# Input products of the state-space branch in single-pass form, from operands split into two parts and stacked to 128 rows through memory

## The chip, the cores and the metric

The kernel runs on one core of a Trainium2 chip. Its engines run in parallel, each in its own program order, and wait for one another on semaphores: TensorE (PE in the profile; its weight loads are PEld), VectorE (DVE), ScalarE (ACT), GpSimd (POOL), and SyncE (SP), which here only issues DMAs. The metric is the device time of one execution in microseconds, lower is better; all times below are in us where nothing else is said.

## The reference

Two transformer-like blocks in float32 run one after the other over 256 tokens with a model width of 2048. The second has three branches: a gated mixer, a state-space branch ("s5") and an attention in stick-breaking form. Their gated sum goes through an output projection, and an MLP of width 8192 follows. The change is in the s5 branch only. It has 64 groups of 16 input channels, each driving 64 complex states:

```python
def s5_mixer(xin, ...):
    u = xin.reshape(bsz, seq, 64, 16)
    ...                                   # a = exp(lam * dt), discretised factors k
    bb_re = k_re[..., None] * b_re - k_im[..., None] * b_im
    bb_im = k_re[..., None] * b_im + k_im[..., None] * b_re
    bu_re = jnp.einsum('blgh,gph->blgp', u, bb_re)
    bu_im = jnp.einsum('blgh,gph->blgp', u, bb_im)
    ...                                   # s[t] = a * s[t-1] + bu[t], complex
    y = (jnp.einsum('blgp,ghp->blgh', s_re, c_re) - jnp.einsum('blgp,ghp->blgh', s_im, c_im))
    y = y.reshape(bsz, seq, 1024) + d * xin
    g = jax.nn.gelu(y)
    return g * jax.nn.sigmoid(g @ w_glu + b_glu)
```

## The kernel before

**Units.** All weight matrices stream through in units: `plan` lists chunks of 512 columns, a chunk has 2 to 8 units, and a unit is 256 rows of weights (512 KB) times 256 tokens. The kernel has 1048 units. For each, SP loads it into `raw` (L377), ScalarE copies it rounded into `whi` (`hi`, L616), VectorE subtracts to get the rest, `wlo` (`lo`, L1121), and TensorE runs 12 matmuls of 128x512 (`unit`, L1735): high by high, high by low and low by high parts, each in a single-pass type (fp32r). All three buffers are rings of four units. SP's load of a unit waits until the split of the unit four before is done, ScalarE's copy waits until TensorE has used the unit four before, and TensorE waits for the split. So the copies and splits run at most four units ahead of TensorE, and the loads four further.

**The order around them.** Everything else is written as generators (`Steps`) that yield a position. On each engine the branch work of position p runs right behind that engine's part of unit p (counted from the first unit of the block's phase), in the order of the list of generators. A position is a place in each engine's program, no time: one engine reaches it earlier than another. In block 2, positions 0 to 95 are the input projections, and the s5 input is ready in two halves: stages are moved by ScalarE (`stage_moves2`, from position 12 and 20 on) and turned by VectorE (`stage_turn2`, positions 20 and 28).

**The s5 branch.** The 32 tiles of 128 states (two groups each) run in 16 pairs m, every `S5D` = 5 positions from `S5Q` = 26. On TensorE `s5_in` (L1878) multiplies at position 26 + 5m: for both parts r (real, imaginary) and both tiles e of the pair, 32 rows of B by 32 rows of the turned input, 256 tokens, in full float32 (which the trace shows as two records a matmul), at the row tile where the operands lie:

```python
ins = mm(PU[e][:, T * r:T * r + T], BT[r][c:c + 32, i, :], XI[c:c + 32, i, :],
         tile_position=(c, 0))
```

VectorE then rotates and scans tile j (`s5`, L1524 to L1532) at `s5_place(j)`: 29 + 5m for the first of a pair and 30 + 5m for the second, behind its split of that unit. It waits for `bu_mm`, which `s5_in` raises. GpSimd rotates back (`block2`, L522 to L525). `s5_out` (L1896) multiplies four tiles of states by C at positions 41 + 10i, so right behind `s5_in` of m = 3, 5 and so on to 15, and once more at 111. SP loads a rotation table for each tile at positions 25 and 30 + 5k (`tables`, L388). From position 72 to 110 the stick-breaking attention runs in the same stage (`attn2`): a head takes 5 positions and goes back and forth between TensorE, ScalarE and VectorE. B is read from memory by GpSimd's queue at the end of block 1, into `BT`. C is scaled by GpSimd (L507 to L512).

Of the kernel before, what the change touches and what calls it, by code (L numbers as in the profile page):

```python
# [21 lines left out]
P = 128  # L22
T = 256
# [26 lines left out]
def build(nc, A, out):  # L50
    with ExitStack() as ctx:
# [197 lines left out]
        BT = [slot(Z, 2 + r).rearrange("p (i c) -> p i c", i=8) for r in range(2)]  # L249
# [21 lines left out]
        GLUQ = [8, 9, 11, 12]  # L271

# [100 lines left out]
        def _(sp_):  # L373
# [6 lines left out]
            def tables():  # L380

                for j in range(S5_TILES):
                    yield S5Q + S5D * (j // 2) + (4 if j % 2 else -1) if j >= NTAB else 6 + j
                    if j == 0:
                        sp_.wait_ge(S("tables_saved"), 32 * S5_TILES // TG)
# [15 lines left out]
            for b in blocks:  # L401
                branch = Steps(tables() if b == 2 else iter(()))
                for ph in "ab":
                    for ch in plan[b, ph]:
                        for i in range(ch.nu):
                            if ch.u0 + i == 0:
                                load_first(ch)
                            else:
                                load(0, ch.u0 + i, ch.w[:, UK * i:UK * i + UK, ch.col:ch.col + CH])
                            if ch.n == 0 and i < 7:  # L410
                                load_pair(i + 1)
                            if 6 <= ch.u0 + i < 6 + NCH:
                                load_x(ch.u0 + i - 6)
                            branch.upto(ch.u0 + i - u0[b, "a"])
                up = rows("w_mlp_up" if b == 1 else "w_mlp_in_2")
# [21 lines left out]
        def _(pool):  # L437
# [46 lines left out]
            def block2():  # L484

                pool.wait_ge(used, mlp_base(1, NF - 1))
                for r in range(2):
                    pool.dma_start(BT[r], A["b_t"][r]).then_inc(S("s5_b_in"), 16)
                for r in range(2):
                    pool.dma_start(CT[r], A["c_t"][r]).then_inc(S("s5_c_in"), 16)  # L490
                pool.dma_start(GW, A["gm_w_t"]).then_inc(S("gm_w_in"), 16)
                pool.wait_ge(evict["dve"], down0[1] + NF * NCH)
                pool.dma_start(A["x1"].rearrange("(t p) n -> p t n", p=P), X).then_inc(S("x_saved"), 16)
                pool.wait_ge(S("gm_w_in"), 16)
# [9 lines left out]
                pool.wait_ge(S("s5_c_in"), 32)  # L504
# [8 lines left out]
                for j in range(S5_TILES):  # L513
# [13 lines left out]
                    if j in (24, 25, 26):  # L527
                        pool.wait_ge(S("z_mm"), 4)
                        if j == 24:
                            pool.dma_start(GMG, A["gm_norm_g_2"][0].partition_broadcast(P)).then_inc(S("gm_gain_in"), 16)  # L530
                        else:
                            load_bias(0, j - 25)
# [4 lines left out]
            def make_tables():  # L537
# [3 lines left out]
                for g in range(S5_TILES // TG):  # L541
                    c, s = TNEW
                    if g:
                        pool.wait_ge(S("tables_saved"), 32 * g)
# [16 lines left out]
                    for i, m in enumerate(TNEW):  # L561
                        pool.dma_start(A["tables"][TG * g:TG * g + TG, :, i, :].rearrange("j p t -> p j t"), m)\
                            .then_inc(S("tables_saved"), 16)
                pool.wait_ge(S("tables_saved"), 32 * S5_TILES // TG)
# [13 lines left out]
            for bi_, b in enumerate(blocks):  # L578
# [4 lines left out]
                if b == 2:  # L583
                    load_biases(3, 5)
                    pool.wait_ge(S("x_saved"), 16)
# [21 lines left out]
        def _(act):  # L607
# [122 lines left out]
            def evictions(b):  # L730
# [4 lines left out]
                for ch in plan[b, "a"] + plan[b, "b"]:  # L735
# [31 lines left out]
                    elif tag == "glu":  # L767
                        act.wait_ge(S("gm_T"), 4)
                        staged(ch, ST[h])
                    else:  # L770
                        if b != blocks[0] and stages == 0:
                            act.wait_ge(S("x_saved"), 16)
# [145 lines left out]
            def s5a():  # L918

                yield S5Q + 88  # L920
                act.wait_ge(S("s5_y"), 8)
                a(GS, GS, ACT.Gelu_apprx_tanh).then_inc(S("s5_g"), 1)
                for h in range(2):
                    yield S5Q + 89 + h
                    act.wait_ge(S("s5_g"), 1)
                    a(YH[:, 8 + 4 * h:12 + 4 * h, :], GS[:, 4 * h:4 * h + 4, :]).then_inc(S("s5_g_hi"), 1)
# [182 lines left out]
        def _(dve):  # L1109
# [446 lines left out]
            def gmlp():  # L1556
# [6 lines left out]
                dve.wait_ge(S("gm_gain_in"), 16)  # L1563
# [17 lines left out]
            def s5_g_lo():  # L1581
                for h in range(2):
                    yield S5Q + 90 + h
                    dve.wait_ge(S("s5_g_hi"), h + 1)
                    tt(YL[:, 8 + 4 * h:12 + 4 * h, :], GS[:, 4 * h:4 * h + 4, :],
                       YH[:, 8 + 4 * h:12 + 4 * h, :].bitcast(F32), ALU.subtract).then_inc(S("s5_g_split"), 1)
# [10 lines left out]
            def mlp(b):  # L1597
# [57 lines left out]
                if b != blocks[-1]:  # L1655
                    dve.wait_ge(S("tables_saved"), 32 * S5_TILES // TG)
# [22 lines left out]
            def gained():  # L1679
                for n in range(2):  # L1680
                    yield (-3, 0)[n]
                    if n == 0:
                        dve.wait_ge(S("gain_in"), 16)
# [6 lines left out]
            for b in blocks:  # L1690
                gens = [Steps(g) for g in (([down_adds(b - 1)] if b != blocks[0] else []) + [x_lo(b, "a"), norm(b, "a"), evictions(b)] + (
                    [stage_turn(), attn1(), attn1_y(), lru(), pool(), sconv(), s5_params()] if b == 1 else [stage_turn2(), s5(), attn2(), s5_g_lo(), gmlp(), glu_out()]) + [merge_turn(b), merge_lo(b)])]
# [38 lines left out]
        def _(pe):  # L1731
# [336 lines left out]
            for b in blocks:  # L2068
# [5 lines left out]
                for ch in plan[b, "a"] + plan[b, "b"]:  # L2074
# [6 lines left out]
                    if ch.tag[0] == "glu":  # L2081
                        pe.wait_ge(S("s5_g_split"), 2)
# [21 lines left out]
def laid_out(v, np):  # L2104
# [18 lines left out]
    m["b_t"], m["c_t"] = bt.reshape(2, P, 8, P), ct.reshape(2, P, 8, P)  # L2123
# [23 lines left out]
```

## Time and profile before

| | us |
|---|---|
| median of 3 runs | 2961.64 |
| lowest and highest | 2961.48 and 3687.77 |
| the profiled execution | 2961.87 |
| its span, from first to last instruction | 2960.1 |
| granted TensorE clock, mean | 1.000 |

The profile is one execution. A row of its timeline has the start, the duration, the engine, the source line, the operation, the names of the written and read tiles, the shape and how many in a row were merged; in brackets stands for how long the engine had been idle and what ended it. Matmuls are pipelined, so the distance of two starts, not the duration, is what one costs. Position p of block 2 is unit p in what follows; its start is the first of its 12 matmuls.

### The profile page before, as it was taken

The numbers are of one execution on the slowest core, as the hardware profiler recorded it, in microseconds if no ns is written. First come the engines' busy times: TensorE is split into PE (matmuls) and PEld (weight loads), VectorE is DVE, ScalarE is ACT, GpSimd is POOL, SyncE is SP. The second block draws the span as 40 slices with busy tenths as digits, with TensorE's granted clock in tenths as the row PEclk, the third lists the DMA queues.
The fourth block names the chain that finished last, engine by engine and source line by source line (L and its number), as shares of the span: only waits on it lengthen the run. The fifth ranks groups of instructions, "written<-read, shape, count | busy, mean of one in ns | idle before, by whom it ended". The sixth has DMA issues, their size and how long they took to land.

```text
span 2960.1 us, 37410 instructions
## 1 busy us (share of the span) xinstructions
PE 2947.3 (100%) x13302; PEld 2429.1 (82%) x13302; DVE 1978.9 (67%) x2104; ACT 1732.3 (59%) x2455; POOL 440.4 (15%) x422
## 2 busy tenths in 40 slices
PE   9999999999999999999999999999999999999998
PEld 7888888888888888888887788888888888888887
DVE  6767654566667777676778886555556666666666
ACT  6776644547655555555675576554557554555555
POOL 1000110110035243320235450110000000000000
PEclk9999999999999999999999999999999999999999
DMA  8656666756666676666765555766665666666664
GB/s 257 182 162 194 198 203 195 199 179 205 191 192 221 191 223 198 217 220 191 261 192 198 194 187 163 217 209 210 203 205 185 200 192 193 193 194 192 192 192 162
DMA packets 298845, 588.43 MB, mean 199 GB/s; under 512 B 18465, under 2 KB 18481, under 8 KB 298353
## 3 DMA queue, kind: packets, MB, share of 16 engines
q1 hardware_dynamic: 292352, 563.61, 61.6%
q0 software_dynamic: 5952, 22.77, 2.4%
q8 instruction: 66, 1.08, 0.1%
q10 hardware_dynamic: 432, 0.62, 0.1%
q14 instruction: 43, 0.34, 0.0%
HBM read 574.35 MB, written 12.58 MB: 198 GB/s over the span
## 4 chain that ended last, share of the span: by engine, by line
PE 95%; ACT 2%; DVE 1%; issue 1%; DMA 0%; SPq 0%; DVEq 0%; ACTq 0%
PE banks L1735 95%; ACT whi L616 1%; ACT L616 0%; PE banks L1738 0%; DVE W L1532 0%; DVE W L1524 0%; DMA raw<-in_w_in 0%; DVE banks L1525 0%; DVE wlo L1121 0%; ACT W L616 0%; DVE banks L1527 0%; ACT G L616 0%; DVE W L1547 0%; DVE W L1220 0%; ACT banks L616 0%
## 5 line engine op out<-in xcount | busy, mean ns | idle before, releaser
L1121 DVE TENSOR_TENSOR wlo<-raw,whi 128x1024 fp32r<-128x1024 f32 x1047 | 1354.1, 1298 | 875.7 <-ACT whi L616 869.2
L616 ACT ACTIVATE whi<-raw 128x1024 fp32r<-128x1024 f32 (+1 forms) x1049 | 1106.7, 1059 | 1041.9 <-PE banks L1735 979.0
L1735 PE MATMUL banks<-whi,Y 128*128 128x512 f32 x4800 | 1484.5, 389 | 0.3 <-DVE W L1220 0.2
L1735 PEld LDWEIGHTS banks<-whi,Y 128*128 128x128 f32 x4800 | 900.9, 188 | 188.3 <-issue 0.9
L1735 PE MATMUL banks<-wlo,Y 128*128 128x512 f32 x2400 | 933.7, 389 | 0.0
L1735 PE MATMUL banks<-whi,XH 128*128 128x512 f32 x1792 | 705.4, 394 | 2.1 <-DVE wlo L1121 1.9
L1735 PE MATMUL banks<-whi,XL 128*128 128x512 f32 x1792 | 698.1, 390 | 0.0
L1735 PE MATMUL banks<-wlo,XH 128*128 128x512 f32 x1792 | 697.6, 389 | 0.0
L1735 PEld LDWEIGHTS banks<-wlo,Y 128*128 128x128 f32 x2400 | 450.5, 188 | 93.2
L1735 PEld LDWEIGHTS banks<-whi,XH 128*128 128x128 f32 x1792 | 336.5, 188 | 78.7 <-issue 8.9
L1735 PEld LDWEIGHTS banks<-whi,XL 128*128 128x128 f32 x1792 | 336.3, 188 | 71.4
L1735 PEld LDWEIGHTS banks<-wlo,XH 128*128 128x128 f32 x1792 | 336.6, 188 | 67.4
L616 ACT ACTIVATE W<-banks 32x256 f32<-32x256 f32 (+1 forms) x532 | 202.4, 381 | 30.0 <-PE banks L1735 20.3
L1667 DVE SCALAR_TENSOR_TENSOR W<-banks,small,W 128x512 f32<-128x512 f32 x256 | 179.8, 743 | 2.2 <-PE banks L1735 2.2
L595 POOL TENSOR_TENSOR W<-W 128x1024 f32<-128x1024 f32 x20 | 63.4, 3172 | 457.9 <-DVE W L1220 457.9
L616 ACT ACTIVATE W<-W 32x256 f32<-32x256 f32 (+3 forms) x254 | 120.0, 473 | 11.4 <-DVE W L1667 3.6
L616 ACT ACTIVATE Z<-W 32x256 f32<-32x256 f32 x208 | 86.2, 414 | 6.1 <-DVE W L1413 3.0
L616 ACT ACT_TABLE_LOAD x41 | 52.6, 1283 | 2.5 <-PEq L2133 1.7
L555 POOL TENSOR_TENSOR W<-G,W 128x128 f32<-128x128 f32 (+3 forms) x16 | 15.8, 989 | 227.7 <-PE banks L1735 227.1
L616 ACT ACTIVATE Y<-W 128x1024 fp32r<-128x1024 f32 (+1 forms) x41 | 41.3, 1006 | 11.1 <-DVE W L1607 10.6
L1602 DVE TENSOR_TENSOR W<-W 128x1024 f32<-128x1024 f32 x32 | 39.2, 1224 | 11.9 <-ACT W L616 11.4
L567 POOL DMA_DIRECT2D W<-in_b_gate x12 | 6.6, 554 | 237.5 <-DVE G L1203 148.4
(256 smaller groups left out, 1191.4 us busy)
## 6 DMA issues: line engine op xcount, KB each, us to landing
raw<-in_w_in SPq DMA_DIRECT2D x383, 512.0 KB, 4.0
raw<-in_w_mlp_up SPq DMA_DIRECT2D x128, 512.0 KB, 3.9
raw<-in_w_mlp_down SPq DMA_DIRECT2D x128, 512.0 KB, 4.1
raw<-in_w_mlp_in SPq DMA_DIRECT2D x128, 512.0 KB, 3.8
raw<-in_w_mlp_out SPq DMA_DIRECT2D x128, 512.0 KB, 3.7
raw<-in_w_branch SPq DMA_DIRECT2D x80, 512.0 KB, 4.4
raw<-in_w_out SPq DMA_DIRECT2D x64, 512.0 KB, 4.5
tables<-G POOLq DMA_DIRECT2D x8, 1024.0 KB, 8.3
```

Of the source, the lines that this page charges most:

```text
L555: tt(a_, c0, pc, ALU.mult)
L567: pool.dma_start(bias_buf(n, k), A["b_gate_2"][0, k, CH * n:CH * n + CH].partition_broadcast(P))\
L595: tt(m, m, TMP[added % 2], ALU.add).then_inc(S("tmp_added"), 1)
L616: return nc.scalar.activation(out_, in_, f, **kw)
L1121: tt(wlo[:, i % RING, :], raw[:, i % RING, :], whi[:, i % RING, :].bitcast(F32), ALU.subtract)\
L1602: tt(HB[1], HB[0], HB[0], ALU.mult).then_inc(S("hidden_ready"), 1)
L1667: return stt(x, PA[n % 2][t], r2[:, t:t + 1], x, ALU.mult, ALU.add)
L1735: return nc.tensor.matmul(out_, l, r, start=start, stop=stop, **kw)
```

## The change

The products of `s5_in` are made in two-part form. B and the s5 input are each split once into a rounded part and the rest; the four combinations are stacked along the contraction, 4 x 32 = 128 rows: [B hi, B hi, B lo, B lo] against [u hi, u lo, u hi, u lo]. A pair m then needs four matmuls of 128x256 in the single-pass type, without a row tile. The stacking is done through memory: the parts are saved to two scratch tensors, and SP fetches the stack of each pair (256 KB of B and twice 128 KB of input) into one of two buffers.

- B comes in as one DMA of 1 MB into `BRAW`, laid out for this. ScalarE makes `BHI` at positions 4 and 5, VectorE `BLO` at 6 and 7; ScalarE makes `UHI` at 21 and 29, VectorE `ULO` at 22 and 31.
- SP gets a second generator, `s5_parts`, behind `tables`: four saves of B (1 MB each) at position 14, eight saves of the first half of the inputs (128 KB each) at 28, a wait for all of these and the first two stacks at 29, eight saves of the second half at 42, and the stack of pair m at position 27 + 5m.
- `s5_in` of m = 0 moves from position 26 to 28; the others stay. VectorE's places don't move.
- Several semaphores are merged (`scratch_saved`, `small2_in`, `gain_in`, `s5_hi`, `s5_lo`).

```diff
-        BT = [slot(Z, 2 + r).rearrange("p (i c) -> p i c", i=8) for r in range(2)]
+        BRAW, BHI, BLO = slot(Z, 2, 2), slot(WR, 6, 2), slot(WR, 8, 2)
+        UIN, UHI, ULO = ([slot(t, i) for i in at] for t, at in ((W, (2, 3)), (WR, (4, 13)), (WR, (5, 5))))
+        SU = [slot(Y, 2)[:, CH * i:CH * i + CH].rearrange("p (e t) -> p e t", e=2) for i in range(2)]
+        SB = [slot(Y, 3)[:, CH * i:CH * i + CH].rearrange("p (r e s) -> p r e s", r=2, e=2) for i in range(2)]
...
+        SAVED = [64, 192, 320]
...
+            def s5_parts():
+
+                yield 14
+                sp_.wait_ge(S("s5_lo"), 2)
+                for part in range(4):
+                    sp_.dma_start(A["s5_b"][:, part].rearrange("m (c x) n -> m c x n", x=4),
+                                  (BHI, BLO)[part // 2].bitcast(F32)).then_inc(S("s5_saved"), 16)
+                yield 28
+                save_inputs(0)
+                yield 29
+                sp_.wait_ge(S("s5_saved"), SAVED[1])
+                load_stack(0)
+                load_stack(1)
+                yield 42
+                save_inputs(1)
+                for m in range(2, 16):
+                    yield S5Q + S5D * m + 1
+                    if m == 8:
+                        sp_.wait_ge(S("s5_saved"), SAVED[2])
+                    sp_.wait_ge(S("bu_mm"), 2 * m - 2)
+                    load_stack(m)
+
+            def save_inputs(h):
+                sp_.wait_ge(S("s5_lo"), 3 + h)
+                for part, m in enumerate((UHI[h], ULO[h])):
+                    for c in range(4):
+                        sp_.dma_start(A["s5_u"][4 * h:4 * h + 4, c // 2, part, :, c % 2, :].rearrange("i c t -> c i t"),
+                                      m[32 * c:32 * c + 32].bitcast(F32).rearrange("p (i t) -> p i t", t=T)).then_inc(S("s5_saved"), 16)
+
+            def load_stack(m):
+                sp_.dma_start(slot(Y, 3)[:, CH * (m % 2):CH * (m % 2) + CH].bitcast(F32),
+                              A["s5_b"][m].rearrange("k c n -> (k c) n")).then_inc(S(f"s5_stack_in{m % 2}"), 16)
+                for d in range(2):
+                    sp_.dma_start(slot(Y, 2)[64 * d:64 * d + 64, CH * (m % 2):CH * (m % 2) + CH].bitcast(F32),
+                                  A["s5_u"][m // 2, m % 2].rearrange("k c e t -> (k c) (e t)"))\
+                        .then_inc(S(f"s5_stack_in{m % 2}"), 16)
...
             def s5a():
 
+                for r in range(2):
+                    yield 4 + r
+                    act.wait_ge(S("s5_b_in"), 16)
+                    a(BHI[:, SL * r:SL * r + SL], BRAW[:, SL * r:SL * r + SL]).then_inc(S("s5_hi"), 1)
+                yield 21
+                act.wait_ge(S("stage_turned2"), 1)
+                a(UHI[0], UIN[0]).then_inc(S("s5_hi"), 1)
+                yield 29
+                act.wait_ge(S("stage_turned2"), 2)
+                act.wait_ge(S("c_scaled"), 1)
+                a(UHI[1], UIN[1]).then_inc(S("s5_hi"), 1)
...
+            def s5_lo():
+                for r in range(2):
+                    yield 6 + r
+                    dve.wait_ge(S("s5_hi"), 1 + r)
+                    c = slice(SL * r, SL * r + SL)
+                    tt(BLO[:, c], BRAW[:, c], BHI[:, c].bitcast(F32), ALU.subtract).then_inc(S("s5_lo"), 1)
+                for h in range(2):
+                    yield (22, 31)[h]
+                    dve.wait_ge(S("s5_hi"), 3 + h)
+                    tt(ULO[h], UIN[h], UHI[h].bitcast(F32), ALU.subtract).then_inc(S("s5_lo"), 1)
...
             def s5_in():
                 for m in range(16):
-                    yield S5Q + S5D * m
-                    i, c0 = m // 2, 64 * (m % 2)
-                    if m == 0:
-                        pe.wait_ge(S("s5_b_in"), 32)
-                        pe.wait_ge(S("stage_turned2"), 1)
-                    else:
-                        if m == 8:
-                            pe.wait_ge(S("stage_turned2"), 2)
+                    yield S5Q + S5D * m + (0 if m else 2)
+                    pe.wait_ge(S(f"s5_stack_in{m % 2}"), 48 * (m // 2 + 1))
+                    if m:
                         pe.wait_ge(S("s5_r_ready"), 2 * m)
                     for r in range(2):
                         for e in range(2):
-                            c = c0 + 32 * e
-                            ins = mm(PU[e][:, T * r:T * r + T], BT[r][c:c + 32, i, :], XI[c:c + 32, i, :],
-                                     tile_position=(c, 0))
+                            ins = mm(PU[e][:, T * r:T * r + T], SB[m % 2][:, r, e, :], SU[m % 2][:, e, :])
                     ins.then_inc(S("bu_mm"), 2)
...
```

## Rows read from the trace of the kernel before

**Rows 1.** PE's row of the page's table: busy time (share of span) x instructions.

```profile
PE 2947.3 (100%) x13302; PEld 2429.1 (82%) x13302; DVE 1978.9 (67%) x2104; ACT 1732.3 (59%) x2455; POOL 440.4 (15%) x422
```

**Rows 2.** The chain that ended last, by engine, shares of the span.

```profile
PE 95%; ACT 2%; DVE 1%; issue 1%; DMA 0%; SPq 0%; DVEq 0%; ACTq 0%
```

**Rows 3.** Timeline of PE: start, duration (us), engine, line, names. Units 30, 31 begin.

```profile
1518.43 0.39 PE L1735 MATMUL banks<-whi,XH 128*128 128x512 f32 x1
...
1521.15 0.39 PE L1735 MATMUL banks<-whi,XH 128*128 128x512 f32 x1
```

**Rows 4.** Timeline of PE around the products of pair m = 0, alone.

```profile
1508.75 0.39 PE L1735 MATMUL banks<-whi,XL 128*128 128x512 f32 x1
1509.07 1.13 PE L1735 MATMUL banks<-W,Z 32*128 32x256 f32 x8
...
1510.47 0.39 PE L1735 MATMUL banks<-wlo,XH 128*128 128x512 f32 x1
```

**Rows 5.** Timeline of PE around pair m = 9 with `s5_out` behind it.

```profile
1645.77 0.39 PE L1735 MATMUL banks<-whi,XL 128*128 128x512 f32 x1
1646.09 1.47 PE L1735 MATMUL banks<-W,Z 32*128 32x256 f32 x10
...
1648.49 0.40 PE L1735 MATMUL banks<-wlo,XH 128*128 128x512 f32 x1
```

**Rows 6.** Timeline of PE around the last `s5_out`, alone between these two.

```profile
1787.77 0.39 PE L1735 MATMUL banks<-whi,XL 128*128 128x512 f32 x1
...
1789.43 0.40 PE L1735 MATMUL banks<-wlo,XH 128*128 128x512 f32 x1
```

**Rows 7.** Timeline of PE around a head's six single-pass matmuls; unit 76 follows.

```profile
1659.76 0.39 PE L1735 MATMUL banks<-whi,XL 128*128 128x512 f32 x1
...
1660.61 0.45 PE L1735 MATMUL banks<-whi,XH 128*128 128x512 f32 x1
1660.89 0.39 PE L1735 MATMUL banks<-wlo,XH 128*128 128x512 f32 x1
```

**Rows 8.** Timeline of ACT: the copies into WR of heads 2 and 4.

```profile
1692.79 0.53 ACT L616 ACTIVATE WR<-W 128x384 fp32r<-128x384 f32 x1 [3.40 <-DVE W L1547]
...
1728.45 0.53 ACT L616 ACTIVATE WR<-W 128x384 fp32r<-128x384 f32 x1 [3.86 <-DVE W L1547]
```

**Rows 9.** Timeline of PE around the same six, two heads on; unit 96 follows.

```profile
1730.17 0.39 PE L1735 MATMUL banks<-whi,XL 128*128 128x512 f32 x1
...
1731.33 0.47 PE L1735 MATMUL banks<-whi,XH 128*128 128x512 f32 x1
```

**Rows 10.** Waits of PE: on whom: us in total, times, longest.

```profile
PE banks L1735 <- DVE wlo L1121: 1.9, 4, 1.2
```

**Rows 11.** Timeline of DVE: scan 0, split of unit 30, split of unit 31.

```profile
1510.25 0.69 DVE L1524 TENSOR_TENSOR W<-banks,G 128x512 f32<-128x512 f32 x1 [1.41 <-PE banks L1735]
...
1513.68 1.23 DVE L1121 TENSOR_TENSOR wlo<-raw,whi 128x1024 fp32r<-128x1024 f32 x1
...
1518.24 1.25 DVE L1121 TENSOR_TENSOR wlo<-raw,whi 128x1024 fp32r<-128x1024 f32 x1
```

**Rows 12.** Windows: length, busy us of PE, PEld, DVE, ACT, POOL; clock, DMA, GB/s.

```profile
1400.00:1500.00 100.00, 99.93 (x456) 82.37 (x456) 71.45 (x73) 62.85 (x103) 21.51 (x13) 1.00 0.75 243
...
1500.00:1650.00 150.00, 150.00 (x733) 117.93 (x732) 129.40 (x168) 88.69 (x131) 78.97 (x72) 1.00 0.62 203
```

**Rows 13.** Timeline of ACT: the copy of unit 15.

```profile
1468.44 1.06 ACT L616 ACTIVATE whi<-raw 128x1024 fp32r<-128x1024 f32 x1 [0.79 <-PE banks L1735]
```

**Rows 14.** Timeline of SP's queue: the issue of load 15.

```profile
1460.66 0.37 SPq L377 DMA_DIRECT2D raw<-in_w_in  x1
```

**Rows 15.** Windows: 2 us in which all DMA engines are full.

```profile
1448.00:1450.00 2.00, 2.00 (x10) 1.68 (x9) 1.23 (x1) 1.08 (x2) 0.00 (x0) 1.00 1.06 396
```

**Rows 16.** DMA issues (page): names, queue, count, KB, median us to landing.

```profile
tables<-G POOLq DMA_DIRECT2D x8, 1024.0 KB, 8.3
...
x<-W POOLq DMA_DIRECT2D x1, 2048.0 KB, 8.3
```

More of the change, by code:

```diff
@@ L384, in tables @@
                     if j == 0:
-                        sp_.wait_ge(S("tables_saved"), 32 * S5_TILES // TG)
+                        sp_.wait_ge(S("scratch_saved"), 32 * S5_TILES // TG)
                     if j >= NTAB:
@@ L402, in _ @@
                 branch = Steps(tables() if b == 2 else iter(()))
+                stacks = Steps(s5_parts() if b == 2 else iter(()))
                 for ph in "ab":
@@ L414, in _ @@
                             branch.upto(ch.u0 + i - u0[b, "a"])
+                            stacks.upto(ch.u0 + i - u0[b, "a"])
                 up = rows("w_mlp_up" if b == 1 else "w_mlp_in_2")
@@ L486, in block2 @@
                 pool.wait_ge(used, mlp_base(1, NF - 1))
+                pool.dma_start(BRAW, A["b_t"]).then_inc(S("s5_b_in"), 16)
                 for r in range(2):
[L488 to L491, printed above, removed]
+                    pool.dma_start(CT[r], A["c_t"][r]).then_inc(S("small2_in"), 16)
+                pool.dma_start(GW, A["gm_w_t"]).then_inc(S("small2_in"), 16)
                 pool.wait_ge(evict["dve"], down0[1] + NF * NCH)
-                pool.dma_start(A["x1"].rearrange("(t p) n -> p t n", p=P), X).then_inc(S("x_saved"), 16)
-                pool.wait_ge(S("gm_w_in"), 16)
+                pool.dma_start(A["x1"].rearrange("(t p) n -> p t n", p=P), X).then_inc(S("scratch_saved"), 16)
+                pool.wait_ge(S("small2_in"), 48)
                 nc.gpsimd.affine_select(out=GW, in_=GW, compare_op=ALU.is_ge, fill=0.0, base=0,
@@ L543, in make_tables @@
                     if g:
-                        pool.wait_ge(S("tables_saved"), 32 * g)
+                        pool.wait_ge(S("scratch_saved"), 32 * g)
                     nc.gpsimd.memset(c[:, :, 0:1], 1.0)
@@ L562, in make_tables @@
                         pool.dma_start(A["tables"][TG * g:TG * g + TG, :, i, :].rearrange("j p t -> p j t"), m)\
-                            .then_inc(S("tables_saved"), 16)
-                pool.wait_ge(S("tables_saved"), 32 * S5_TILES // TG)
+                            .then_inc(S("scratch_saved"), 16)
+                pool.wait_ge(S("scratch_saved"), 32 * S5_TILES // TG)
             def load_bias(n, k):
@@ L584, in _ @@
                     load_biases(3, 5)
-                    pool.wait_ge(S("x_saved"), 16)
+                    pool.wait_ge(S("scratch_saved"), 32 * S5_TILES // TG + 16)
                 for n in range(NCH):
@@ L771, in evictions @@
                         if b != blocks[0] and stages == 0:
-                            act.wait_ge(S("x_saved"), 16)
+                            act.wait_ge(S("scratch_saved"), 32 * S5_TILES // TG + 16)
                         if stages >= 2:
@@ L925, in s5a @@
                     act.wait_ge(S("s5_g"), 1)
-                    a(YH[:, 8 + 4 * h:12 + 4 * h, :], GS[:, 4 * h:4 * h + 4, :]).then_inc(S("s5_g_hi"), 1)
+                    a(YH[:, 8 + 4 * h:12 + 4 * h, :], GS[:, 4 * h:4 * h + 4, :]).then_inc(S("s5_hi"), 1)
             def attn2():
@@ L1562, in gmlp @@
                 chain(nc.vector.reciprocal(grs, grs))
-                dve.wait_ge(S("gm_gain_in"), 16)
+                dve.wait_ge(S("gain_in"), 16)
                 for t in range(NT):
@@ L1655, in mlp @@
                 if b != blocks[-1]:
-                    dve.wait_ge(S("tables_saved"), 32 * S5_TILES // TG)
+                    dve.wait_ge(S("scratch_saved"), 32 * S5_TILES // TG)
                 hidden_lo(NF - 1, 1)
@@ L1682, in gained @@
                     if n == 0:
-                        dve.wait_ge(S("gain_in"), 16)
+                        dve.wait_ge(S("gain_in"), 32)
                     dve.wait_ge(evict["dve"], down0[blocks[-1]] + 4 * (NF - 1) + n + 1)
@@ L2081, in _ @@
                     if ch.tag[0] == "glu":
-                        pe.wait_ge(S("s5_g_split"), 2)
+                        pe.wait_ge(S("s5_lo"), 6)
                     lh, ll = (XH, XL) if ch.lhs == "X" else (YH, YL)
@@ L2122, in laid_out @@
             ct[r, q, :, :, :, q, :] = c[:, :, q].transpose(3, 0, 1, 2)
-    m["b_t"], m["c_t"] = bt.reshape(2, P, 8, P), ct.reshape(2, P, 8, P)
+    m["b_t"] = bt.reshape(2, 2, 2, 32, 8, P).transpose(4, 1, 3, 0, 2, 5).reshape(P, 2 * SL)
+    m["c_t"] = ct.reshape(2, P, 8, P)
     return m
@@ L2141 @@
     aps["tables"] = nc.dram_tensor("tables", (32, 128, 2, T), _mybir.dt.float32, kind="Internal").ap()
+    aps["s5_b"] = nc.dram_tensor("s5_b", (16, 4, 32, CH), _mybir.dt.float32, kind="Internal").ap()
+    aps["s5_u"] = nc.dram_tensor("s5_u", (8, 2, 2, 32, 2, T), _mybir.dt.float32, kind="Internal").ap()
     aps["x1"] = nc.dram_tensor("x1", (T, D), _mybir.dt.float32, kind="Internal").ap()
```

10 lines of the change are left out of this document (4 added, 6 removed).

## The prediction

> **What bounds the kernel now.** I read the page's engine table first, then its chain of work: TensorE is busy for the whole span, and 95% of the chain is its stream matmuls [rows 1, 2]. So the sum to make is of TensorE's time: what it no longer has to do, plus every moment in which it comes to stand. One unit (12 matmuls of 128x512) takes 2.72 us, from the starts of units 30 and 31, or 0.227 a matmul [rows 3]. Then the timeline of TensorE around the edited products. For one tile pair m, eight records of 32x256 lie between the last matmul before and the second after, which are 1.72 us apart where two stream gaps would be 0.45: a lone group costs 1.27 us [rows 4]. For m = 3, 5 ... 15 the output products of `s5_out` follow in the same gap, and both cost 2.72 - 0.45 = 2.27 [rows 5]; `s5_out` alone (its last call) costs 1.66 - 0.45 = 1.21 [rows 6].
>
> **The products.** The new form has four single-pass matmuls of 128x256 over 128 rows, with four weight sets. The trace has no group of exactly that shape; the nearest is attention's six single-pass matmuls of 1024 columns in all, with changing weights: 1.13 - 0.45 = 0.68 us, 0.113 each [rows 7]. Four make 0.45 us, and they have the same 1024 columns, so between 0.45 and 0.68 I take 0.45. A lone group saves 1.27 - 0.45 = 0.82. In a shared gap the entry into the two-pass form now falls on `s5_out`: 2.27 - 0.45 - 1.21 = 0.61. Nine lone and seven shared groups: 7.4 + 4.3 = 11.7 us, if nothing waits.
>
> The Trainium skill ("TensorE: Matmul & The Clock Gate", section "Part 3: Packing small matmuls — row/col tiling") says that matmuls at different row tiles run concurrently, with a measured 3.07 times for four of 32 rows; that speaks against giving the tiles up. By it the old pairs cost little more than half of untiled ones; the rows price the packed form directly, and the sum doesn't change.
>
> **What is kept of it.** From position 76 on, TensorE shares the stage with the stick-breaking heads, and there it isn't alone in setting the time. ScalarE's copy into WR for heads 2 and 4 is 35.66 us apart [rows 8]. Between them ScalarE and VectorE work through a chain of table loads, exponentials, scans and splits in program order, and TensorE already waits for it: the gap ahead of unit 96 is 1.16 us where the same gap ahead of unit 76 is 0.85 [rows 7, 9], and 1.9 us in four waits for VectorE's wlo stand in its list of waits [rows 10]. None of the edited work is in that chain. A TensorE that is faster by 1.43 us per two heads only waits longer. So the savings of m = 10 to 15 are lost, and those of m = 0 to 9 stay: 6 x 0.82 + 4 x 0.61 = 7.4 us.
>
> **The moved first product.** m = 0 goes from behind unit 26 to behind unit 28, but VectorE keeps its places: scan 0 between the splits of units 29 and 30, scan 1 between those of 30 and 31. Before, scan 0 began at 1510.25, the split of unit 30 at 1513.68, that of 31 at 1518.24, ending 1519.49 [rows 11], and TensorE began those units at 1518.43 and 1521.15 [rows 3]. Now: unit 27 begins at 1508.98, 28 ends at 1514.42, the products at 1514.9 plus 0.2 for their last drain. Scan 0 from 1515.1 takes 3.43, the split of unit 30 takes 1.23: 1519.8. TensorE ended unit 29 at 1517.6 and stands for 2.2 us. Scan 1 and the next split end 1519.49 - 1514.91 = 4.6 us later, a unit lasts 2.72: it stands for another 1.85. Behind them now comes the split of the second half of the inputs (1.2 us), so scan 2 begins some 1.6 to 2.1 us behind its product, where unit 36 has a slack of about as much (unit 31's was 1521.15 - 1519.49 = 1.66): 0 to 0.5 more, I take 0.3. VectorE is busy for 129.4 of 150 us in this stage [rows 12], with idle time of about 1 us a pair, so the lag fades over three or four pairs instead of growing. Sum: 4.3 us lost.
>
> **The splits.** ScalarE gets four copies of 128x1024 (1.06 us each, as its copy of unit 15 [rows 13]) and VectorE four subtractions (1.23). Those of B stand at positions 4 to 7, those of the inputs at 21, 22, 29 and 31. Between 1400 and 1500 VectorE is busy for 71% and ScalarE for 63% [rows 12], and the splits run up to four units, 10.9 us, ahead of TensorE: cost 0 there, and the last one is in the sum above. If that cover were gone, each would cost its 1.1 to 1.2 us.
>
> **The way through memory.** SP's queue carries the weights, so every byte and wait on it counts. (1) Behind load 14 it now issues four saves of B, 4.19 MB. Load 15, issued at 1460.66 [rows 14], queues behind them. Rates: 396 GB/s is moved when all engines are full [rows 15]; the save of x, 2.1 MB in 8.3 us to landing, is 250; a save of tables, 1.05 MB in 8.3 us, is 126, beside other traffic [rows 16]. I take 396, since this save has runs of 8 KB and the queue to itself: 10.6 us from 1459.5, 1.3 for load 15, 1 to land: 1472.4. ScalarE's copy, so far at 1468.44, comes 4 us late; copy and split end between 1474.7 and 1476.0. Unit 15 begins at 1518.43 - 1.27 - 15 x 2.72 = 1476.4. So it is just hidden: 0. At 250 GB/s the saves last 6.2 us longer and TensorE stands for some 4 to 5 us; at 126 GB/s, 22.6 longer and some 20. (2) Behind load 28 SP issues eight saves of 128 KB, waits for them behind load 29, and issues six loads: 14 issues at 0.37 and a landing of 3 to 4 us hold load 30 back by about 4. Its split isn't wanted before 1518.5: 0. The stacks land by about 1508, the product wants them at 1514.4: 0. (3) Three loads a pair, 0.5 MB and 1.1 us of issue in every 13.6 us; the second saves at position 42 delay load 43 by some 3 us, with twice that to spare: 0. Their wait for `bu_mm` is for a product TensorE did ten units earlier.
>
> The Trainium skill ("DMA: Bandwidth & Descriptors", section "Anatomy of one DMA — SWDGE (gpsimd) path") puts most of a transfer's fixed 2 us on the receipt of the last write, slowest for HBM, and gives 2.0 us + bytes / 436 GB/s. By it the four saves would be through in 11.6 us, and the sum stands.
>
> POOL's DMAs carry the same bytes, and the merged semaphores count things that are done in the same order: 0.
>
> **Sum.** -7.4 + 4.3 = -3.1 us. The profiled execution took 2961.87 us for a span of 2960.1; the median is 2961.64, the same within 0.3. Forecast: 2961.64 - 3.1 = 2958.5 us.
>
> **Rivals.**
> (a) Full gain. VectorE takes the new place of m = 0 without a stall, or the heads' chain moves up with TensorE: 2961.6 - 11.7 + 4.3 = 2954.2 with one of them, 2950 with both. For it: I read the chain as free of TensorE from idle gaps alone. Against: program order fixes scan 0 ahead of the split of unit 30. Chance 0.17.
> (b) Slower than before. The saves of B hold load 15 longer than the splits' lead. It decides from a landing at about 1474, that is a rate under some 340 GB/s; at 250 the time is 2958.5 + 4.5 = 2963, at 126 GB/s 2978. For it: both measured saves landed slower. Against: they ran beside other traffic. Chance 0.25, most of it near 2963.
> (c) VectorE bounds the pairs. It needs 129.4 of 150 us, and TensorE's own time falls by 7 us there; with the lag of the first pairs kept alive by slower scans beside POOL, m = 1 to 9 give nothing: -0.8 + 4.3, 2965. Against: TensorE's units fall by 5%, VectorE has 14% idle. Chance 0.1.
> My sum holds to within about 2 us with 0.48.
>
> **Range and chances.** 2951 to 2967 takes in (a), most of (b) and (c). 2% of this kernel, about what its measurement can tell from no change, is 59 us: neither 11.7 us of gain nor 20 us of the slowest saves come near. Within 2%: 0.98; faster 0.005, slower 0.015, for a wait on SP that I haven't seen.
>
> **What would show it.** TensorE's timeline: four records in about 0.45 us per pair, 0.82 off a lone gap. TensorE waits for VectorE's wlo ahead of units 30 and 31, 2.2 and 1.9 us, and for little before. The copy of unit 15 released by a DMA, near 1472. The gaps of heads 2 to 4 still 35.7 us apart, with longer waits of TensorE in that stage. I am wrong if units 30 and 31 start on time, if unit 15 waits, or if the WR copies come closer together.

## The result: the changed kernel is slower, by 13 us

| | median us | runs | profiled execution | its span |
|---|---|---|---|---|
| before | 2961.82 | 2961.48 to 3687.77, 6 runs | 2961.87 | 2960.1 |
| changed | 2974.68 | 2973.11 to 2977.95, 6 runs | 2973.11 | 2971.4 |

The ratio is 1.0045 with a 95% interval of 1.0035 to 1.0054. The forecast was 2958.5 us with a range of 2951 to 2967: the sign is wrong, and the time lies 7.7 us above the range. The run of 3687.77 us here and one of 4231.58 us in an experiment below lie far above all the others of their kernels, and the ratios leave them out.

**The page of the changed kernel** shows the sort of loss in two lines that answer to [rows 1, 2]: TensorE's share of the chain fell from 95% to 93%, and transfers stand in the chain with 1%.

```profile
PE 2940.6 (99%) x13238; PEld 2431.0 (82%) x13238; DVE 1981.1 (67%) x2108; ACT 1736.1 (58%) x2459; POOL 441.7 (15%) x421
...
PE 93%; DVE 2%; ACT 2%; issue 2%; DMA 1%; SPq 0%; DVEq 0%; ACTq 0%
```

**Whom TensorE waits for**, over the whole kernel (us in total, times, longest). The wait for wlo has grown against [rows 10], and above it stands one that the kernel before doesn't have:

```profile
PE banks L1796 <- DMA Y<-s_u: 10.4, 1, 10.4
PE banks L1796 <- DVE wlo L1173: 8.8, 11, 2.0
```

**Where it is lost.** The starts of the units of block 2, changed kernel less kernel before, from TensorE's timelines of the two profiled executions:

| unit | 14 | 15 | 26 | 27 | 29 | 30 | 31 | 32 | 36 | 37 | 38 | 76 | 111 |
|---|---|---|---|---|---|---|---|---|---|---|---|---|---|
| later by, us | 0.05 | 2.10 | 2.25 | 1.10 | 1.43 | 3.62 | 5.50 | 4.99 | 5.41 | 15.98 | 17.38 | 12.66 | 11.32 |

So 2.1 us are lost at unit 15, 4.1 at units 30 and 31, and 12.0 at units 37 and 38. What the shorter products give back from unit 38 to 76 is 4.7 us.

**Units 37 and 38.** TensorE's timeline of the changed kernel (start, duration, engine, line, operation; in brackets the idle time before it and what released it). The Y line is the product group of m = 2:

```profile
1544.08 0.39 PE L1796 MATMUL banks<-whi,XL 128*128 128x512 f32 x1
1554.88 1.23 PE L1796 MATMUL banks<-Y 128*128 128x256 f32 x4 [10.41 <-DMA Y<-s_u]
1555.90 0.63 PE L1796 MATMUL banks<-whi,XH 128*128 128x512 f32 x1
1556.33 0.63 PE L1796 MATMUL banks<-wlo,XH 128*128 128x512 f32 x1
...
1559.46 0.40 PE L1796 MATMUL banks<-whi,XH 128*128 128x512 f32 x1
```

The operands of m = 2 weren't there. SP's queue in the same stretch says why:

```profile
1543.69 1.52 SPq L381 DMA_DIRECT2D raw<-in_w_in  x2
1545.25 4.54 SPq L420 DMA_DIRECT2D s_u<-WR  x8
1549.84 0.46 SPq L424 DMA_DIRECT2D Y<-s_b  x1
1550.34 1.10 SPq L427 DMA_DIRECT2D Y<-s_u  x2
1551.49 0.58 SPq L424 DMA_DIRECT2D Y<-s_b  x1
1552.12 1.08 SPq L427 DMA_DIRECT2D Y<-s_u  x2
1553.24 0.59 SPq L381 DMA_DIRECT2D raw<-in_w_in  x1
```

The loads of the stack of m = 2 (the first Y lines, 1549.84 to 1551.44) are issued behind load 42 and behind the eight saves of the second half, and those of m = 3 right after them. TensorE had wanted m = 2 at 1544.47. The text of the generator has it so: in `s5_parts`, `yield 42` and `save_inputs(1)` stand ahead of the loop whose first turn, m = 2, yields 37. A generator hands out its work in the order of its text (`Steps` goes on while the yielded position is at or below the one reached), so a position below one already passed is "at once", and 37 became 42. Had the text's number 37 held, the loads would have gone out five loads earlier.

After the wait TensorE is also slow: matmuls start 0.43 us apart until 1558.89 instead of 0.23. The granted clock there is 0.50 (the third number from the end in the first row below), the lower of the two levels, 1.2 of 2.4 GHz. Seven of them lose 1.4 us, and the product group takes 1.02 us from start to next start instead of 0.47. The whole stage has a granted clock of 0.97 where [rows 12] had 1.00, and TensorE's busy time lacks 14 us:

```profile
1556.00:1558.00 2.00, 2.00 (x6) 1.56 (x6) 1.82 (x4) 0.00 (x0) 0.00 (x0) 0.50 0.72 239
...
1500.00:1650.00 150.00, 135.65 (x635) 110.02 (x634) 121.12 (x157) 84.56 (x127) 71.42 (x64) 0.97 0.73 233
```

**Unit 15.** Against [rows 13], ScalarE's copy of its weights starts 7.6 us later and is released by the transfer:

```profile
1476.07 1.06 ACT L657 ACTIVATE whi<-raw 128x1024 fp32r<-128x1024 f32 x1 [8.37 <-DMA raw<-in_w_in]
```

The issues on SP in front of it, where [rows 14] had load 15 at 1460.66, and the traffic (columns as in [rows 12]):

```profile
1458.41 5.23 SPq L399 DMA_DIRECT2D s_b<-WR  x4
1463.68 4.13 SPq L381 DMA_DIRECT2D raw<-in_w_in  x3
```

```profile
1460.00:1462.00 2.00, 2.00 (x11) 1.65 (x10) 1.41 (x2) 1.66 (x3) 2.00 (x1) 1.00 1.02 292
...
1466.00:1468.00 2.00, 2.00 (x10) 1.65 (x9) 1.68 (x2) 1.66 (x3) 2.00 (x1) 1.00 1.01 418
```

**Units 30 and 31** stand as forecast: TensorE waits for VectorE's split, and in front of the split stands scan 0 of the moved product.

```profile
1516.67 0.64 PE L1796 MATMUL banks<-Y 128*128 128x256 f32 x4
1522.05 0.50 PE L1796 MATMUL banks<-whi,XH 128*128 128x512 f32 x1 [2.00 <-DVE wlo L1173]
1526.65 0.51 PE L1796 MATMUL banks<-whi,XH 128*128 128x512 f32 x1 [1.56 <-DVE wlo L1173]
```

### The profile page after: what moved, and what is told of

The parts are those of the page before. It is cut to its first block, busy times and chain, and to the rows that moved or that the text cites. A ratio compares the mean times of both kernels' runs of the same rounds, so it can differ in the third digit from the quotient of the medians.

```text
span 2971.4 us, 37372 instructions
## 1 busy us (share of the span) xinstructions
PE 2940.6 (99%) x13238; PEld 2431.0 (82%) x13238; DVE 1981.1 (67%) x2108; ACT 1736.1 (58%) x2459; POOL 441.7 (15%) x421
## 4 chain that ended last, share of the span: by engine, by line
PE 93%; DVE 2%; ACT 2%; issue 2%; DMA 1%; SPq 0%; DVEq 0%; ACTq 0%
PE banks L1796 93%; ACT whi L657 1%; DMA raw<-in_w_in 1%; DVE wlo L1173 1%; ACT L657 0%; PE banks L1799 0%; DVE W L1584 0%; DVE W L1576 0%; DVE banks L1577 0%; DVE banks L1579 0%; ACT W L657 0%; SPq L420 0%; ACT G L657 0%; DMA Y<-s_u 0%; DVE W L1599 0%
## 5 line engine op out<-in xcount | busy, mean ns | idle before, releaser
L657 ACT ACTIVATE Y<-W 128x1024 fp32r<-128x1024 f32 (+1 forms) x41 | 41.2, 1006 | 11.1 <-DVE W L1668 10.6
```

Of the source, the lines that this page charges most:

```text
L657: return nc.scalar.activation(out_, in_, f, **kw)
```

## Experiments

The theory after the first look: four independent things add up. The shorter products give about 7 us, the moved m = 0 costs 4 to 5, the saves of B cost 2, and SP's order of the second half costs some 12. The rivals: a stall elsewhere takes over as soon as one is removed (VectorE or the queue is full), or the shorter products bring little in truth. Where a shift of a unit is given below, the starts in one profiled execution are compared with those in the profiled execution of before.

**The products alone.** The edit, in the kernel before (TensorE's generator of the products, every m):

```
-ins = mm(PU[e][:, T*r:T*r+T], BT[r][c:c+32, i, :], XI[c:c+32, i, :], tile_position=(c, 0))
+ins = mm(PU[e][:, T*r:T*r+T], XH[:, 4*(m%4)+2*r+e, 0:P], XL[:, e, :])
```

> The kernel before with only TensorE's part changed: four single-pass matmuls of 128x256 over 128 rows per pair, all at their old positions, with operands that lie ready (rows of the normalised input, so the values in this branch are not the reference's); no splits, saves or fetches are added. Theory A (the gain of m = 0 to 9 is kept, the heads' stage returns only some 1.3 us, as between the two profiles): 6 x 0.80 + 4 x 0.59 + 1.3 = 8.5 us less, 2953.3 us. Rival B (the heads' stage gives back nothing): 2954.6 us. Rival C (all is kept): 11.7 less, 2950.1 us.

Measured: 2953.62 us (2952.89 to 2954.81, 8 runs) against 2961.38, ratio 0.9973 (0.9963 to 0.9984). By unit 72 it is 7.23 us ahead, ten groups, and at the end 6.97 (0.12 of both stand there from the first units on). So the prices of the products hold. In this execution the heads' stage gives back all that its six groups save; the medians, 7.8 us apart, lie between theories A and B and can't tell them apart. The lone group reads as foretold, of 0.93 us from the first start to the last below, where the same two are 1.72 apart in [rows 4], so 0.79 less:

```profile
1508.63 0.39 PE L1735 MATMUL banks<-whi,XL 128*128 128x512 f32 x1
1508.85 0.64 PE L1735 MATMUL banks<-XL,XH 128*128 128x256 f32 x4
1509.33 0.40 PE L1735 MATMUL banks<-whi,XH 128*128 128x512 f32 x1
1509.56 0.40 PE L1735 MATMUL banks<-wlo,XH 128*128 128x512 f32 x1
```

**The products and the move.** As above, with m = 0 two positions later:

```
-yield S5Q + S5D * m
+yield S5Q + S5D * m + (0 if m else 2)
```

> As e3_products, with the product of m = 0 at position 28 instead of 26. Theory A (VectorE's fixed places make units 30 and 31 late by 2.2 and 1.9 us): 4.1 us above e3_products, about 2957.4 us. Rival B (the late units of the changed kernel come from its transfers and splits, not from the move): within 0.5 us of e3_products.

Measured: 2958.41 us (2957.38 to 2959.07, 10 runs), ratio 0.9989 (0.9979 to 0.9999). The move costs 4.8 us between the medians; in the profile unit 31 starts 2.90 behind that of before, where with the products alone it is 0.92 ahead, and by unit 72 the two kernels are 4.0 us apart. Theory A stands, and one that has VectorE take the new place for nothing falls.

**The heads' stage alone.** The new products only for m of 10 or more:

```
+if m >= 10:
     ins = mm(PU[e][:, T*r:T*r+T], XH[:, 4*(m%4)+2*r+e, 0:P], XL[:, e, :])
```

> The kernel before, where TensorE's products of the groups m=10 to 15 alone take the new form, at their old positions, on operands that are ready (the values of this branch are left wrong; splits, saves and fetches are not there). It asks whether the heads' stage keeps anything. Theory A (the stage is a chain of its own between the copies of two heads and gives back whatever arrives early, and all of what it is saved): end 0, median 2961.4. Theory B (the products in the heads' stage are on the chain in part): the six groups keep the 1.3 us seen in the changed kernel, 2960.1. Theory C (they count in full, 6 x 0.7 us): 2957.2.

Measured: 2961.79 us (2960.40 to 4231.58, 11 runs), ratio 1.0001 (0.9992 to 1.0010). The 4.2 us of theory C are excluded. Zero and 1.3 us can't be told apart by the medians. From unit 76 to unit 111 the profiled execution keeps 1.0 of them, the changed kernel's 1.3, that of the products alone none. The ten profiled executions with new products fall into two sorts. Five keep 1.0 to 1.4 us in that stage: this one, those of the changed kernel and of the products with the move, and below those with only m = 2 put in order and with later scans. The other five keep nothing, or lose 0.2 to 0.4. What decides it isn't shown. A difference of about 1.5 us between two profiled executions' ends can come from this alone.

**SP's order for m = 2.** In the changed kernel, the saves of the second half go behind the stack of m = 2 and stay at 42:

```
-yield 42
-save_inputs(1)
 for m in range(2, 16):
+    if m == 3:
+        yield 42
+        save_inputs(1)
     yield S5Q + S5D * m + 1
```

> The changed kernel, except that SP fetches the stack of pair m = 2 behind load 37 (with the saves of the second half of the inputs still at 42) instead of behind load 42. Theory A (program order): the 10.4 us in which TensorE waits for this stack, and the 1.4 us that unit 37 then takes longer at the lower clock, go away: about 2963 us, and no wait for a DMA in TensorE's list. Rival B (the way through memory is too slow as such: bandwidth or latency of the saved and fetched parts): TensorE waits for this or the next stack nearly as long, 2970 us or more.

Measured: 2966.92 us (2964.57 to 2970.08, 10 runs), ratio 1.0017 (1.0008 to 1.0027), so 7.8 us of the 13 are gone with a change of order alone. That is 4 us above theory A's number, but rival B's wait for a stack isn't there. The wait for s_u isn't in TensorE's waits any more, and the clock is full. Not all of the 12.4 us came back: a stall appears at units 45 and 46, TensorE's timeline of this kernel:

```profile
1572.99 0.50 PE L1797 MATMUL banks<-whi,XH 128*128 128x512 f32 x1 [1.24 <-DVE wlo L1174]
1577.65 0.50 PE L1797 MATMUL banks<-whi,XH 128*128 128x512 f32 x1 [1.63 <-DVE wlo L1174]
```

In the changed kernel TensorE comes to that place some 9 us later in its trace, so that the load was in time there (this is argued from the starts alone). (The profiled execution of this kernel also started block 2 late: 2.45 us are gone at unit 0, before any of the edited work, and the shifts are read without them.)

**The saves of B apart.** In the changed kernel, one save each behind loads 14, 16, 18 and 20:

```
-yield 14
-sp_.wait_ge(S("s5_lo"), 2)
 for part in range(4):
+    yield 14 + 2 * part
+    if part == 0:
+        sp_.wait_ge(S("s5_lo"), 2)
     sp_.dma_start(...)
```

> The changed kernel, except that the four saves of B are issued behind loads 14, 16, 18 and 20 instead of all behind load 14. Theory A (4 MB in front of load 15 on SP's queue): the 2.1 us by which unit 15 starts late go away, 2972.6 us. Rival B (the added copies and subtractions of B make the splits late): unit 15 is late as before, 2974.7 us.

Measured: 2972.72 us (2969.99 to 2973.74, 6 runs), ratio 1.0035 (1.0022 to 1.0048). Unit 15 starts 0.16 us behind that of before instead of 2.10, and no other unit up to 26 waits, so theory A holds for the place of the loss. That the end comes earlier by as much is not shown. The median is 2.0 us less than the changed kernel's, 1.5 with each beside its own runs of before, but the two intervals of the ratio overlap. And the profiled execution, with its unit 15 in time, ends 0.6 us later than the changed kernel's (spans of 2972.0 and 2971.4): it loses 13.1 us instead of 12.0 at units 37 and 38, where its wait for the stack is 10.73 us long, and the heads' stage keeps nothing of what the changed kernel's keeps.

**Both orders.** The two edits together:

> The changed kernel with both orders of SyncE mended: the stack of m=2 stands behind load 37, and the four saves of the splits of B stand one by one behind loads 14, 16, 18 and 20. Theory A (the two stalls are independent): 2966.9 less the 2.0 us that the spread saves gave alone, 2964.9; the stall of 3.35 us at units 45 and 46 stays. Theory B (what arrives early is waited out at units 45 and 46 or in the heads' stage): as with the order alone, 2966.9.

Measured: 2962.21 us (2961.57 to 2966.01, 11 runs), ratio 1.0003 (0.9994 to 1.0012). That is 4.7 us below the kernel with m = 2 mended, where theory A has 2.0. The profiled executions, each without its own start, are 3.2 us apart at unit 76 (2.9 of them arose at units 15 and 16, where the one with m = 2 mended loses more than the changed kernel) and 1.8 at the end, since the heads' stage keeps 1.3 us of one and none of the other. That 1.8 is near theory A's 2.0 is therefore luck. Theory B falls by the medians, although one part of it, time given back in the heads' stage, is seen in these two executions. The other 2.9 us between the medians I can't place.

**The second half's saves apart.** Nothing but the eight saves at 43, 45, ... 57:

```
+def save_second():
+    for i in range(8):
+        yield 43 + 2 * i
+        save_inputs(1, range(i, i + 1))
```

> As the kernel with both orders, and the eight saves of the second half of the inputs stand one by one behind loads 43, 45 ... 57 instead of together behind load 42. Theory A (the 3.35 us at units 45 and 46 come from load 43, which waits in SyncE's order behind the eight saves): 3.3 us less than the kernel with both orders, about 2961.5. Theory B (they come from VectorE, whose scans and copies are late there): no difference.

Measured: 2960.12 us (2957.77 to 2960.59, 11 runs), ratio 0.9993 (0.9984 to 1.0002). The medians are 2.1 us apart, the shift at unit 46 shows 3.0: 4.70 us behind with both orders, 1.70 with the saves apart. The wait at units 45 and 46 is gone, so it came through load 43, as the two queues show. With both orders:

```profile
1542.96 5.17 SPq L422 DMA_DIRECT2D s_u<-WR  x8
1548.17 0.44 SPq L426 DMA_DIRECT2D Y<-s_b  x1
...
1549.79 1.10 SPq L381 DMA_DIRECT2D raw<-in_w_in  x2
```

With the saves apart, the load after the stack goes out 5.5 us earlier:

```profile
1542.63 0.47 SPq L430 DMA_DIRECT2D Y<-s_b  x1
1543.15 1.09 SPq L433 DMA_DIRECT2D Y<-s_u  x2
1544.28 0.59 SPq L381 DMA_DIRECT2D raw<-in_w_in  x1
1544.91 0.47 SPq L426 DMA_DIRECT2D s_u<-WR  x1
```

A late load reaches TensorE two units on by way of VectorE. In the kernel with both orders ScalarE's copy of unit 43 waits for it, and VectorE's split for the copy:

```profile
1555.30 1.06 ACT L659 ACTIVATE whi<-raw 128x1024 fp32r<-128x1024 f32 x1 [4.37 <-DMA raw<-in_w_in]
```

```profile
1556.39 1.23 DVE L1175 TENSOR_TENSOR wlo<-raw,whi 128x1024 fp32r<-128x1024 f32 x1 [1.84 <-ACT whi L659]
1559.50 1.22 DVE L1175 TENSOR_TENSOR wlo<-raw,whi 128x1024 fp32r<-128x1024 f32 x1 [1.88 <-ACT whi L659]
```

VectorE stands 3.7 us there, and all its later work, transpose, scans and the splits of units 45 and 46 in program order, is late by that; with the saves apart it doesn't stand at these splits, and its transpose begins 3.7 us earlier (1556.91 instead of 1560.64).

**The scans later.** On top of that, VectorE's scans 0 and 1 go behind the splits of two more units, and its split of the second half one position earlier (with a wait for the saves of the first half, which are done by then):

```
-return S5Q + S5D * (j // 2) + 3 + j % 2
+return S5Q + S5D * (j // 2) + (3 if j > 1 else 5) + j % 2
-yield (22, 31)[h]
+yield (22, 30)[h]
```

> As the kernel with spread saves, and VectorE's scans of the first product stand at positions 31 and 32 instead of 29 and 30, its copy of the second half at 30. Theory A (the stalls of 2.2 and 1.9 us at units 30 and 31 are scans of VectorE that stand in front of the splits of units 30 and 31): they go in large part, 3 to 4 us less than with spread saves, about 2958. Theory B (any place for the scans on this full engine costs the same): no difference, about 2961.5.

Measured: 2957.25 us (2955.52 to 2960.34, 11 runs), ratio 0.9988 (0.9979 to 0.9997), 2.9 us less than with the saves apart, where theory A has 3 to 4. The scans and the split of the second half were moved together; what each brings isn't told apart. The units 30 and 31 start without a wait, 0.91 us ahead of before where they were 1.00 and 2.86 behind. TensorE then waits at one place for scan 1 and at one for a split (1.00 us at unit 36):

```profile
1514.30 0.64 PE L1806 MATMUL banks<-Y 128*128 128x256 f32 x4
...
1524.55 0.71 PE L1806 MATMUL banks<-Y 128*128 128x256 f32 x4 [1.43 <-DVE W L1592]
```

**The second product later, too.** m = 1 goes behind unit 32:

```
-yield S5Q + S5D * m + (0 if m else 2)
+yield S5Q + S5D * m + (2, 1)[m] if m < 2 else S5Q + S5D * m
```

> As the kernel with later scans, and TensorE's product group of m=1 stands behind unit 32 instead of 31. In the kernel with later scans TensorE waits 1.43 us there for scan 1 of VectorE, and 1.00 us for the split of unit 36. Theory A (a stall at one place that the later place avoids): 1.4 us less, about 2955.8. Theory B (VectorE is full through units 32 to 36, and what TensorE doesn't wait at 31 it waits at units 33 to 36): no difference, 2957.2, and the wait ahead of unit 36 grows to 2.4 us.

Measured: 2957.75 us (2956.60 to 2959.77, 11 runs), ratio 0.9987 (0.9978 to 0.9996): no difference. The wait at m = 1 is gone and stands at units 35 and 36 instead, as theory B has it (0.52 and 2.08 are 2.6 us, where 1.43 and 1.00 were 2.4):

```profile
1525.66 0.64 PE L1806 MATMUL banks<-Y 128*128 128x256 f32 x4
1532.28 0.50 PE L1806 MATMUL banks<-whi,XH 128*128 128x512 f32 x1 [0.52 <-DVE wlo L1181]
1537.37 0.50 PE L1806 MATMUL banks<-whi,XH 128*128 128x512 f32 x1 [2.08 <-DVE wlo L1181]
```

VectorE's timeline shows no idle time over 0.04 us between 1518.6 and 1537 in the kernel with later scans. I read it so: as long as the work for m = 0 begins two units late and that for m = 2 doesn't, 2.4 us are lost, wherever they are shown. The kernel with later scans is the fastest of those that do all of the work: 4.3 us under the kernel before, 17.4 under the changed one.

## Why the prediction was wrong, step by step

**What held.** TensorE was the bound, and the sum was rightly one of its time. The products: a lone group saved 0.82 by the prediction and 0.80 in the changed kernel, a shared one 0.61 and 0.59, and the ten groups that count 7.4 and 7.2. The moved product: 2.2 and 1.85 at units 30 and 31, measured 2.2 and 1.9; by the medians the whole move costs 4.8 instead of 4.3, and the products give 7.8 instead of 7.4. Those two terms by themselves give 2958.4 us on the chip, the forecast's own number, in part because the two misses cancel.

**The step that failed** is (3) under "The way through memory", "Three loads a pair ...: the second saves at position 42 delay load 43 by some 3 us, with twice that to spare: 0. Their wait for `bu_mm` is for a product TensorE did ten units earlier". I asked what the saves delay among the weight loads and whether their own wait is met, and took the positions in the code as the positions of the work. What the saves hold up is the next item of the same generator, the stack of m = 2, whose number 37 lies below the 42 ahead of it. The product needs the stack at unit 36, SP issues it at unit 42's load: 10.41 us of waiting, 2.0 more at the lower clock in and after the group. Nothing in the rows of before shows it; the diff does, to one who writes down SP's list of issues in order with TensorE's need beside each. The rule that I wrote at the head of the sum, every moment in which TensorE comes to stand, was not asked of the stacks beyond m = 1.

The second half of the same sentence failed too, though that was hidden: "with twice that to spare". In the kernels with the order of m = 2 mended, saves and stack hold load 43 by 5.5 us (by 3 in the prediction), and that costs 3.0 to 3.4 us at units 45 and 46. The spare time was counted at load 43's own unit, and there it was right; it was VectorE that had none, since it does its scans of the same pair behind that split.

**The saves of B**, step (1), were sized too low: the prediction has load 15 landed at 1472.4, and it landed 12.36 us behind its issue, at 1476.04. By rival (b) it is decided at a landing of about 1474, and what was lost is 2.05 us, half of rival (b)'s 4 to 5.

```profile
1463.68 12.36 DMA raw<-in_w_in
```

The term mis-sized is the number of bytes ahead of the landing, more than the rate. The nine windows of 2 us from 1458 to 1476 moved 248 to 418 GB/s, 356 in the mean and 6.4 MB in all. Of these, 4.19 MB are the four saves, in packets of 8 KB, and 2.2 MB are loads. I had counted the saves and load 15 (0.5 MB) alone. But load 14 had gone out 0.4 us ahead of the saves, and it and load 13 were still moving: the first 3 us have 0.77 MB and no packet of 8 KB. And the last 3 us, again without one, moved 1.08 MB, twice load 15: loads 16 and 17, issued 1.5 and 2.9 us behind it, landed only 1.3 and 2.6 us behind it, so they shared the engines with it. My 10.6 us for the saves plus 1.3 for the load, with 2.2 MB instead of the load's 0.5, would have put the landing 4.3 us behind 1472.4, and it was 3.6 us behind. The page's rows of the changed kernel's own transfers, beside [rows 16], show that landings took longer than the load's usual 4.1 us:

```profile
s_b<-WR SPq DMA_DIRECT2D x4, 1024.0 KB, 10.4
Y<-s_b SPq DMA_DIRECT2D x16, 256.0 KB, 5.7
Y<-s_u SPq DMA_DIRECT2D x32, 128.0 KB, 6.0
...
s_u<-WR SPq DMA_DIRECT2D x16, 128.0 KB, 3.8
```

The prediction drew on the Trainium skill ("DMA: Bandwidth & Descriptors", "Anatomy of one DMA — SWDGE (gpsimd) path") for an estimate of 11.6 us for the four saves. That section is on transfers that GpSimd issues, and its formula is for one DMA; these went out on SP's queue with loads before and behind. Here the last of the four was issued at 1461.34 and took 12.3 us, so that from the first issue at 1458.41 all four took 15.2 us, 3.6 more than the estimate.

**Step (2)**, the first half's saves at load 28, cost nothing at load 30's own unit, as foretold, although it held load 30 back by 11 us (1511.69 against 1500.70) and not by 4. Its 8 saves and 6 loads took 5.2 and 4.9 us of issue and not 14 x 0.37:

```profile
1498.26 5.22 SPq L420 DMA_DIRECT2D s_u<-WR  x8
...
1508.67 2.98 SPq L427 DMA_DIRECT2D Y<-s_u  x2
1511.69 1.61 SPq L381 DMA_DIRECT2D raw<-in_w_in  x3
```

**The heads' stage** was said to keep nothing. It keeps 1.0 to 1.4 us of 4.2 in five profiled executions and nothing in five, as told above. In the changed kernel the copies into WR of heads 2 and 4 are 35.36 us apart, where 35.66 was foretold ([rows 8]); the wait in front of them is for VectorE as before:

```profile
1705.43 0.53 ACT L657 ACTIVATE WR<-W 128x384 fp32r<-128x384 f32 x1 [4.77 <-DVE W L1599]
...
1740.79 0.53 ACT L657 ACTIVATE WR<-W 128x384 fp32r<-128x384 f32 x1 [5.13 <-DVE W L1599]
```

**The whole sum** of the profiled executions: -7.2 for the products up to m = 9, -1.3 behind them, +2.1 for unit 15, +4.1 for the move, +10.4 for the stack, +2.0 for the clock make 10.1 us. The span grew by 11.3; the other 1.2 us are in pieces of 0.1 to 0.4, of which the largest is at unit 36. Between the medians the difference is 12.9 us; the changed kernel's six runs lie over 4.8 us, and the profiled one is the fastest of them.

With both orders mended and the saves apart, splits, saves and fetches themselves still cost 1.6 us between medians (2960.12 with them, 2958.41 without, each beside its own runs of before) and 0.9 by unit 76 of the profiled executions, which the prediction had at 0.

**The rivals.** (a) the full gain, didn't come: neither half did. (b) came in part, as 2.05 of the 13 us at unit 15. (c), VectorE as the bound, is true of units 30 to 36 alone (2.4 to 4.3 us), and the pairs behind them give their savings in full. The chance of 0.25 for the other side was meant for the wrong place: the loss had its seat in SP's order and not in a rate. That the time stayed within 2% of the kernel before, given 0.98, came true, but no part of the mechanism hangs on it.

## What to carry to other kernels

Where one queue's work comes from several generators with positions, write down the issues in the order in which they leave, and beside each the moment at which its reader wants it; a number that is lower than the one ahead of it is not a position. A transfer that rides in the weight queue is to be split into single ones between the loads: that took away the 2.05 us of waiting at unit 15 for the saves of B, and the 3 us at units 45 and 46 (2.1 between the medians) for those of the second half. How much of the first reaches the end of the kernel is not clear. And when spare time is counted for a late load, count it for every engine that has the load's data in its program order, not for TensorE alone.

## What the runs showed of the hardware that was new to me

SP's issue of one load, 0.37 us in [rows 14], became longer behind the saves of B: 5.23 us for the four saves of 1 MB and 4.13 us for the three loads behind them, 1.4 each. So the time of an issue is no constant that could be multiplied. Full DMA engines alone don't do it: the next load took 0.37 us again, in a window (1468 to 1470) with the engines at 1.00 and 418 GB/s, as much as in any of the nine.

```profile
1469.43 0.37 SPq L381 DMA_DIRECT2D raw<-in_w_in  x1
```

What makes an issue long is not shown.

After 10.4 us without work TensorE had a granted clock of 0.50 for 4.0 us, from 1554.88 to 1558.89; the row of the wait shows 10.41 us and the loss is 12.4. Behind the waits of 1.6 and 2.0 us in the same kernel only the first matmul is longer (0.50 instead of 0.39).

A stall that is taken away uncovers others: the 12.4 us gave 7.8. What is open: why the runs of the changed kernel and of the one with m = 2 mended lie over 4.8 and 5.5 us where 25 runs of before lie over 2.6, why the two mended orders together bring 2.9 us more in the medians than in the two profiled executions, what the saves of B cost at the end of the kernel, and what decides whether the heads' stage keeps its 1.0 to 1.4 us.
